# Final sums of the experts' outputs with 64 tokens' two choices on 128 partitions, and the last normalisation on three engines

## The chip, the cores and the metric

One core of a Trainium2 chip. The metric is the device time of one launch in microseconds; the median over the runs counts. All matrices are float32. Engines: PE (TensorE), DVE (VectorE), ACT (ScalarE), POOL (GpSimd) and SP, which issues most DMAs.

## What is computed

One decoder layer for 544 tokens of width 1024: 512 of a prompt and 32 of eight samples, with shared weights. Three mixers (a gated short convolution, a Mamba-2 scan, a cross-attention) are merged and projected, then normalised. The second half is a mixture of 32 experts in 4 groups, two experts per token, and a second normalisation:

```python
    x = layer_norm(ALPHA * x + mix, ln1_g[l], ln1_b[l])
    ffn = hier_moe(x.reshape(b * L, D_MODEL), ...)
    x = layer_norm(ALPHA * x + ffn, ln2_g[l], ln2_b[l])
...
    # hier_moe, its end
    out = lax.map(expert_block, (buf.reshape(n_blocks, MOE_BLOCK, D_MODEL), block_expert)).reshape(-1, D_MODEL)
    y = jnp.sum(out[dest].reshape(T, EXP_TOPK, D_MODEL).astype(f32) * gate[..., None], axis=1)
```

So every token's result is ALPHA times its own row of x, plus gate 0 times the output of its first expert, plus gate 1 times that of its second, normalised over its 1024 columns: minus the mean, over the standard deviation, times ln2_g, plus ln2_b. ALPHA is 2 to the power of one quarter.

## The kernel before

The kernel is written by hand, one program per engine, with semaphores between them. Tokens lie in five tiles: tiles 0 to 3 with 128 prompt tokens each, tile 4 with the 32 samples' tokens. The stages in order are: a stream of weight slabs, each split into a high and a low part (ACT and DVE) for three PE products; the scan; the cross-attention; the output projection with the first normalisation; the router; the experts; the final sum and second normalisation.

**Router.** DVE works out gates, slots and indices (to L2250). It signals gi_v (indices for POOL's gathers), slot_v (what SP and later the other engines read), and gate_v (gates, for ACT). `gate[:, t, k]` is the gate of token t*128 + p for its choice k.

**Experts.** There are 64 fixed blocks of 32 tokens (NB0 = 64) over 32 experts, and 28 more that are skipped unless an expert gets more tokens than planned. An expert's weights are two halves of w1 (2 MB each) and w2 (2 MB). SP loads them one expert after another into three places of `arena`: fetch1 (L545) waits until PE has done the gate products (gu_mm) of the expert three before, fetch2 (L551) until it has done its down products (dn_mm). Per block POOL gathers the tokens' rows (L1542, an indirect DMA), PE transposes them (turn_x, L1074), ACT copies them (L1468), PE multiplies by w1 (gate_up, L1090: 32 instructions in four column sets of 32), ACT computes the SiLU (L1473), DVE the product (hidden, L2258), PE turns it (turn_h, L1097), DVE copies (L2262), PE multiplies by w2 (down, L1109), DVE copies (L2268), and POOL scatters (L1554) into ybuf in DRAM. ybuf has four rows of 256 columns for each pair of token and choice, pair 2*token + choice.

After the copies of the third block ACT writes `gd`, eleven matrices of 128x128 (L1484, L1485): for every tile and choice the identity with its rows scaled by that gate, and the identity times ALPHA. PE needs them only behind the last block.

**The end.** SP waits for ov_p, which POOL raises when all scatters have landed (L1589), and then loads each tile from ybuf with one token's two outputs side by side on a partition, 8 KB (L603, into yld); the fifth load waits until PE has used a slot, since four semaphores serve five tiles. PE forms each half of a tile (512 columns, one PSUM bank) as three products in one sum: ALPHA identity times x (own_part, L1138), gate 0 times the first output (L1154), gate 1 times the second (L1155). An fp32 matmul appears as two passes in the records. Own parts of tiles 0 and 1 come before ov_p, those of tiles 2 and 3 behind it, the one of tile 4 when DVE has read tile 0 from PSUM. Then, per tile in the order 0 to 4:

```python
                    c_.done(v.bn_stats(lstat[0:n, t, half], pair_[:, half]))          # L2295, twice
                v.bn_aggr(lmv[0:n, t], ...).then_inc(Z["f_a"], 1)                     # L2297
                v.scalar_tensor_tensor(halves(x1[0:n, t]), pair_, lmv[0:n, t, 0:1], halves(lnw2[0:n, 0]), ALU.subtract, ALU.mult)  # L2302
                c_.done(v.reciprocal(lrs[0:n, t:t + 1], lsd[0:n, t:t + 1]))           # L2305
                v.scalar_tensor_tensor(x1[0:n, t], x1[0:n, t], lrs[0:n, t:t + 1], lnw2[0:n, 1], ALU.mult, ALU.add)                 # L2308
```

All five are DVE's. ACT gives the standard deviation in between (a square root of one column, L1502). SP stores each tile when f_p says that it is done (L608). SP's order is: all loads, then all stores.

Of the kernel before, what the change touches and what calls it, by code (L numbers as in the profile page):

```python
# [69 lines left out]
W1S, W2S = KT * D, FF // P * D  # L70
SKIP = 2048
# [5 lines left out]
C_QUAD, C_SKIP, C_PART, C_KEYC, C_CAP, C_START, C_VAL, C_MEAN = 790, 791, 792, 793, 794, 795, 798, 800  # L77
# [28 lines left out]
def build(nc, A):  # L106
    with ExitStack() as ctx:
# [187 lines left out]
        yld = place("yld", [P, TT, 2 * D], F32, r_hi)  # L295
        gd = place("gd", [P, 2 * TT + 1, P], F32, tmp_at)
# [6 lines left out]
        raw_half = sem("raw_half")  # L303
        w_hi = sem("w_hi")
# [23 lines left out]
                 "g_in0 g_in1 g_in2 g_in3 sc_out0 sc_out1 cur cur_ov fin_in0 fin_in1 fin_in2 fin_in3 gate_v gd_a f_mm f_v f_a f_sd f_p f_st ov_p on").split()  # L328
# [35 lines left out]
        def _(sp_):  # L364
# [250 lines left out]
        def _(pe):  # L615
# [496 lines left out]

            turn_x(0, 0)
# [3 lines left out]
            for n_ in range(1, NB0):  # L1117
# [4 lines left out]
                turn_h(n_)  # L1122
            down(NB0 - 1)
# [36 lines left out]
        def _(act):  # L1160
# [338 lines left out]
            for t in range(TT):  # L1499
                n = min(T, t * P + P) - t * P  # L1500
                act.wait_ge(Z["f_a"], t + 1)
                nc.scalar.activation(lsd[0:n, t:t + 1], lmv[0:n, t, 1:2], ACT.Sqrt, bias=small[0:n, 41:42]).then_inc(Z["f_sd"], 1)  # L1502


        @block.gpsimd
        def _(pool):
# [82 lines left out]
            pool.sem_inc(Z["ov_p"], 1)  # L1589


        @block.vector
        def _(dve):
# [655 lines left out]
            dve.sem_inc(Z["slot_v"], 1)  # L2249
            dve.sem_inc(Z["gate_v"], 1)  # L2250
# [39 lines left out]
            for t in range(TT):  # L2290
                n = min(T, t * P + P) - t * P
                pair_ = ps[0:n, 2 * (t % 4):2 * (t % 4) + 2, :]
                for half in range(2):
                    dve.wait_ge(Z["f_mm"], 2 * t + half + 1)
# [3 lines left out]
                dve.wait_ge(Z["f_a"], t + 1)  # L2298
# [137 lines left out]
```

## Time and profile before

| | |
|---|---|
| time, median of 3 runs | 1616.73 us |
| runs | 1616.74, 1616.73, 1613.91 us |
| span of the profiled execution, first to last instruction | 1610.5 us |
| mean granted clock of TensorE | 0.964 |
| PE busy | 1487.6 us, 92% |
| DVE busy | 691.9 us, 43% |
| ACT busy | 453.1 us, 28% |
| POOL busy | 176.2 us, 11% |
| DMA moved | 368.25 MB, mean 229 GB/s |
| chain that ended last | PE 72%, DMA 18%, DVE 5%, ACT 2% |

The profile gives no time of the profiled execution other than its span; the median of the runs is 6.2 us longer than that span. Times in views are microseconds from the start of the span, durations of single instructions in groups are ns. "x" is a count of instructions, "idle before" the time in which the engine had nothing to do ahead of them, with what ended it; the granted clock is a share of 2.4 GHz. DMA share is the mean busy share of the 16 DMA engines.

### The profile page before, as it was taken

The numbers are of one execution on the slowest core, as the hardware profiler recorded it, in microseconds if no ns is written. First come the engines' busy times: TensorE is split into PE (matmuls) and PEld (weight loads), VectorE is DVE, ScalarE is ACT, GpSimd is POOL, SyncE is SP. The second block draws the span as 40 slices with busy tenths as digits, with TensorE's granted clock in tenths as the row PEclk, the third lists the DMA queues.
The fourth block names the chain that finished last, engine by engine and source line by source line (L and its number), as shares of the span: only waits on it lengthen the run. The fifth ranks groups of instructions, "written<-read, shape, count | busy, mean of one in ns | idle before, by whom it ended". The sixth has DMA issues, their size and how long they took to land.

```text
span 1610.5 us, 34696 instructions
## 1 busy us (share of the span) xinstructions
PE 1487.6 (92%) x14388; PEld 1194.2 (74%) x14388; DVE 691.9 (43%) x1227; ACT 453.1 (28%) x874; POOL 176.2 (11%) x356
## 2 busy tenths in 40 slices
PE   7999999999899999999999989958987887898897
PEld 7999999999788999999988769744543443444443
DVE  5766666676679572223444325562111111111115
ACT  4534553544222452123343333112100000000000
POOL 1100000000000000000000000003423232333320
PEclk9999999999899999999999999978989998999989
DMA  5223354344448323252355453775999999999994
GB/s 201 75 82 92 115 160 151 113 126 157 152 149 298 116 80 102 83 216 91 118 194 189 177 220 99 285 331 221 418 423 423 420 422 421 397 403 420 420 409 177
DMA packets 86849, 368.25 MB, mean 229 GB/s; under 512 B 14296, under 2 KB 37536, under 8 KB 71712
## 3 DMA queue, kind: packets, MB, share of 16 engines
q1 hardware_dynamic: 80576, 357.37, 58.5%
q0 software_dynamic: 6144, 8.95, 1.5%
q8 instruction: 106, 1.74, 0.4%
q14 instruction: 23, 0.19, 0.0%
HBM read 344.81 MB, written 29.31 MB: 232 GB/s over the span
## 4 chain that ended last, share of the span: by engine, by line
PE 72%; DMA 18%; DVE 5%; ACT 2%; issue 2%; SPq 1%; DVEq 0%; POOLq 0%; POOL 0%; ACTq 0%
PE ps L628 35%; DMA arena<-in_w 16%; PE ps L1090 8%; PE ps L772 5%; PE ps L1109 4%; PE ps L986 3%; PE ps L877 3%; PE ps L859 3%; PE ps L723 1%; PE ps L720 1%; PE ps L909 1%; PE ps L888 1%; PE ps L1074 1%; DVE wl L1604 1%; PE ps L713 1%
## 5 line engine op out<-in xcount | busy, mean ns | idle before, releaser
L1090 PE MATMUL ps<-arena,xT 128*32 128x256 f32 x4096 | 259.5, 406 | 62.6 <-DMA arena<-in_w 62.0
L1604 DVE TENSOR_TENSOR wl<-raw,wh 128x1024 fp32r<-128x1024 f32 x151 | 183.4, 1222 | 169.2 <-ACT wh L1167 168.9
L1090 PEld LDWEIGHTS ps<-arena,xT 128*32 128x32 f32 x4096 | 133.3, 116 | 164.9 <-issue 51.8
L628 PE MATMUL ps<-xh,wh 128*128 128x272 f32 x1136 | 243.6, 296 | 3.2 <-DVE wl L1604 2.0
L628 PE MATMUL ps<-xh,wl 128*128 128x272 f32 x1136 | 235.0, 288 | 0.0
L628 PE MATMUL ps<-xl,wh 128*128 128x272 f32 x1136 | 234.2, 288 | 0.0
L628 PEld LDWEIGHTS ps<-xh,wh 128*128 128x128 f32 x1136 | 179.1, 188 | 14.1 <-issue 9.7
L628 PEld LDWEIGHTS ps<-xl,wh 128*128 128x128 f32 x1136 | 178.4, 188 | 0.0
L628 PEld LDWEIGHTS ps<-xh,wl 128*128 128x128 f32 x1136 | 177.4, 189 | 0.0
L1167 ACT ACTIVATE wh<-raw 128x1024 fp32r<-128x1024 f32 x151 | 158.1, 1055 | 38.7 <-PE ps L986 20.7
L2258 DVE TENSOR_TENSOR hbuf<-sg,ps 128x128 f32<-128x128 f32 x64 | 18.4, 288 | 311.7 <-ACT sg L1473 311.7
L1473 ACT ACTIVATE sg<-ps 128x128 f32<-128x128 f32 x64 | 17.8, 278 | 422.1 <-PE ps L1090 422.1
L1109 PE MATMUL ps<-arena,hTb 128*32 128x256 f32 x2048 | 124.6, 384 | 1.1 <-DMA arena<-in_w 1.1
L1526 POOL MEMSET xg<- 128x256 f32 x4 | 1.1, 312 | 890.8 <-PE ps L986 890.8
L1109 PEld LDWEIGHTS ps<-arena,hTb 128*32 128x32 f32 x2048 | 60.5, 110 | 45.6 <-issue 11.7
L1179 ACT ACTIVATE tmp<-ps 128x544 f32<-128x544 f32 x56 | 34.6, 617 | 191.5 <-PE ps L628 180.2
L2268 DVE COPY yb<-ps 128x256 f32<-128x256 f32 x64 | 27.2, 425 | 112.0 <-PE ps L1109 112.0
L1554 POOL DMA_INDIRECT ybuf_dram<-yb,curs x64 | 65.6, 1025 | 59.1 <-POOL curs L1551 55.7
L1542 POOL DMA_INDIRECT xg<-x_dram,curg x60 | 62.8, 1047 | 51.0 <-POOL curg L1536 51.0
L772 PE MATMUL ps<-xh,wh 128*128 128x272 f32 x256 | 55.3, 298 | 0.0
L772 PE MATMUL ps<-xl,wh 128*128 128x272 f32 x256 | 53.3, 290 | 0.0
L772 PE MATMUL ps<-xh,wl 128*128 128x272 f32 x256 | 53.1, 289 | 0.0
(408 smaller groups left out, 2348.7 us busy)
## 6 DMA issues: line engine op xcount, KB each, us to landing
arena<-in_w SPq DMA_DIRECT2D x96, 2048.0 KB, 30.5
raw<-in_slabs SPq DMA_DIRECT2D x151, 512.0 KB, 4.3
bc<-acs_dram SPq DMA_DIRECT2D x16, 512.0 KB, 5.8
hs<-in_h SPq DMA_DIRECT2D x16, 512.0 KB, 5.2
out_h_sample<-hs SPq DMA_DIRECT2D x16, 512.0 KB, 4.8
kv<-in_kT SPq DMA_DIRECT2D x8, 1024.0 KB, 4.9
kv<-in_vc SPq DMA_DIRECT2D x4, 1024.0 KB, 7.1
kvx<-in_vc SPq DMA_DIRECT2D x2, 2048.0 KB, 11.0
```

Of the source, the lines that this page charges most:

```text
L628: r = nc.tensor.matmul(ps[:, 2 * (ub % 2) + half, 0:HT], w[:, s, col], x[:, koff + kk, half * HT:half * HT + HT], start=first and kk == 0 ...
L772: r = nc.tensor.matmul(ps[:, 2 * (u % 2) + half, 0:HT], w[:, b % RING, kk * P:kk * P + P], x[:, kk, half * HT:half * HT + HT], start=kk == ...
L859: r = nc.tensor.matmul(ps[:, 4 * what + 2 * m + half, :], a[:, kk, m * P:m * P + P], w[:, b % RING, half * 512:half * 512 + 512], start=kk ...
L877: r = nc.tensor.matmul(ps[:, 2 * (u % 2) + half, 0:HT], w[:, b % RING, kk * P:kk * P + P], x[:, kk, half * HT:half * HT + HT], start=kk == ...
L986: r = nc.tensor.matmul(ps[0:n, bank, :], a[:, k, t * P:t * P + n], w[:, b % RING, kq * 512:kq * 512 + 512], start=k == 0 and n_ == 0, stop ...
L1090: r = nc.tensor.matmul(ps[QS * c:QS * c + QS, 2, 0:2 * FQ], xT[:, s, kk % 2, kk // 2 * QS:kk // 2 * QS + QS], arena[:, at_:at_ + 2 * FQ], ...
L1109: r = nc.tensor.matmul(ps[QS * q_:QS * q_ + QS, 5, 0:QD], hTb[:, QS * c:QS * c + QS], arena[:, at_:at_ + QD], start=c == 0, stop=c == NQ - 1)
L1167: nc.scalar.activation(wh[:, b % RING], raw[:, b % RING], ACT.Copy).then_inc(w_hi, 1)
L1179: nc.scalar.activation(tmp[:, ub % RING, 0:T].rearrange("p (h t) -> p h t", h=2), pair(ub), func).then_inc(evac, 1)
L1542: nc.gpsimd.indirect_dma_start(out=xg[s][:], out_offset=None, in_=A["x1d"], in_offset=bass.IndirectOffsetOnAxis(ap=gidx[:, s:s + 1] if cnt ...
L1554: nc.gpsimd.indirect_dma_start(out=A["ybuf"], out_offset=bass.IndirectOffsetOnAxis(ap=curs[:, s:s + 1], axis=0), in_=yb[:, s], in_offset=N ...
L1604: v.tensor_tensor(wl[:, s], raw[:, s], wh[:, s].bitcast(F32), ALU.subtract).then_inc(w_lo, 1)
```

## The change

The order of tiles in the end is now 4, 0, 1, 2, 3 (LAST), everywhere: loads, own parts, sums, normalisation, stores. ybuf is read as pairs: 128 partitions hold both choices of 64 tokens (2 x 64 pairs), in two groups per tile, with 4 KB each. A sum over a token's two choices is then one product with 128 rows and 64 columns; the two groups of a tile write to PSUM partitions 0 to 63 and 64 to 127. For the 32 samples one group with 64 rows and 32 columns is enough. The five loads have semaphores of their own (four that were used at the start of the kernel, and raw_half), and the fifth waits for nothing.

The matrix for it has the gate of pair r in row r and column r // 2. DVE writes its transpose (gl), in five instructions between slot_v and gate_v; PE transposes it (five transposes, behind turn_h of block 1); ACT copies the result from PSUM (two copies) and writes the ALPHA identity.

Of the normalisation, DVE keeps statistics, the first pass and the reciprocal. For the first four tiles in order ACT multiplies by the reciprocal (in place) and POOL adds ln2_b; for the last tile DVE does both in one pass as before, once POOL's four adds are done.

```diff
+PG = P // 2
+LAST = (TT - 1, *range(TT - 1))
...
-        yld = place("yld", [P, TT, 2 * D], F32, r_hi)
-        gd = place("gd", [P, 2 * TT + 1, P], F32, tmp_at)
+        yld = place("yld", [P, TT, 2, D], F32, r_hi)
+        gd = place("gd", [P, TT + 1, P], F32, tmp_at)
+        gl = place("gl", [P, TT, P], F32, tmp_at + 4 * (TT + 1) * P)
+        fin_in = [*x_in, raw_half]
...
         # SP
-            for t in range(TT):
-                if t >= 4:
-                    sp_.wait_ge(Z["f_mm"], 2 * (t - 3))
-                n_ = min(T, t * P + P) - t * P
-                sp_.dma_start(yld[0:n_, t], rows(A["ybuf"].rearrange("(t k) d -> t (k d)", k=2 * NQ), t)
-                              ).then_inc(Z[f"fin_in{t % 4}"], 16)
-            for t in range(TT):
-                sp_.wait_ge(Z["f_p"], t + 1)
+            for i, t in enumerate(LAST):
+                pairs_ = A["ybuf"].rearrange("(p q) d -> p (q d)", q=NQ)[2 * t * P:2 * min(T, t * P + P)]
+                if t < TT - 1:
+                    sp_.dma_start(yld[:, t], pairs_.rearrange("(g p) d -> p g d", p=P)).then_inc(fin_in[i], 16)
+                else:
+                    sp_.dma_start(yld[0:2 * SAMP, t, 0], pairs_).then_inc(fin_in[i], 16)
+            for i, t in enumerate(LAST):
+                sp_.wait_ge(Z["f_p"], i + 1)
...
         # PE
+            def turn_gates():
+                pe.wait_ge(Z["gate_v"], 1)
+                for t in range(TT - 1):
+                    nc.tensor.transpose(ps[:, 6, t * P:t * P + P], gl[:, t], ident)
+                nc.tensor.transpose(ps[0:2 * SAMP, 7, 3 * P:3 * P + SAMP], gl[0:SAMP, TT - 1, 0:2 * SAMP], ident[0:SAMP, 0:SAMP]
+                                    ).then_inc(Z["gt_mm"], 1)
...
                 turn_h(n_)
+                if n_ == 1:
+                    turn_gates()
...
-            for t in range(TT):
+            for i, t in enumerate(LAST):
                 n = min(T, t * P + P) - t * P
-                pe.wait_ge(Z[f"fin_in{t % 4}"], 16 * (t // 4 + 1))
-                if t >= 4:
-                    pe.wait_ge(Z["f_v"], t - 3)
-                    own_part(t)
+                if i >= 4:
+                    pe.wait_ge(Z["f_v"], i - 3)
+                    own_part(i)
+                pe.wait_ge(fin_in[i], 32)
                 for half in range(2):
-                    out, c = ps[0:n, 2 * (t % 4) + half, :], half * 512
-                    nc.tensor.matmul(out, gd[0:n, 2 * t, 0:n], yld[0:n, t, c:c + 512], start=False, stop=False)
-                    nc.tensor.matmul(out, gd[0:n, 2 * t + 1, 0:n], yld[0:n, t, D + c:D + c + 512], start=False, stop=True
-                                     ).then_inc(Z["f_mm"], 1)
+                    c = half * 512
+                    for r0 in range(0, n, PG):
+                        m = min(PG, n - r0)
+                        r = nc.tensor.matmul(ps[r0:r0 + m, 2 * (i % 4) + half, :], gd[0:2 * m, t, r0:r0 + m],
+                                             yld[0:2 * m, t, r0 // PG, c:c + 512], start=False, stop=True)
+                    r.then_inc(Z["f_mm"], 1)
...
         # ACT
-            for t in range(TT):
-                for k in range(2):
-                    nc.scalar.activation(gd[:, 2 * t + k], ident, ACT.Copy, scale=gate[:, t, k:k + 1])
-            nc.scalar.activation(gd[:, 2 * TT], ident, ACT.Copy, scale=ALPHA).then_inc(Z["gd_a"], 1)
+            act.wait_ge(Z["gt_mm"], 1)
+            nc.scalar.activation(gd[:, 0:TT - 1], ps[:, 6, :].rearrange("p (t q) -> p t q", q=P), ACT.Copy)
+            nc.scalar.activation(gd[0:2 * SAMP, TT - 1, 0:SAMP], ps[0:2 * SAMP, 7, 3 * P:3 * P + SAMP], ACT.Copy)
+            nc.scalar.activation(gd[:, TT], ident, ACT.Copy, scale=ALPHA).then_inc(Z["gd_a"], 1)
...
                 nc.scalar.activation(lsd[0:n, t:t + 1], lmv[0:n, t, 1:2], ACT.Sqrt, bias=small[0:n, 41:42]).then_inc(Z["f_sd"], 1)
+                if i < TT - 1:
+                    act.wait_ge(Z["f_v"], i + 1)
+                    act.wait_ge(Z["f_r"], i + 1)
+                    nc.scalar.activation(x1[0:n, t], x1[0:n, t], ACT.Copy, scale=lrs[0:n, t:t + 1]).then_inc(Z["f_n"], 1)
...
         # POOL
+            for i, t in enumerate(LAST[:-1]):
+                n = min(T, t * P + P) - t * P
+                pool.wait_ge(Z["f_n"], i + 1)
+                nc.gpsimd.tensor_tensor(x1[0:n, t], x1[0:n, t], lnw2[0:n, 1], ALU.add).then_inc(Z["f_p"], 1)
...
         # DVE, between slot_v and gate_v
+            for t in range(TT):
+                c_.done(v.scalar_tensor_tensor(gl[:, t].rearrange("p (m k) -> p m k", k=2),
+                                               riota[:, 0, 0:PG].unsqueeze(2).to_broadcast([P, PG, 2]), cst[:, C_OWN:C_OWN + 1],
+                                               gate[:, t].unsqueeze(1).to_broadcast([P, PG, 2]), ALU.is_equal, ALU.mult))
+            c_.sync()
...
         # DVE, per tile
-                c_.done(v.reciprocal(lrs[0:n, t:t + 1], lsd[0:n, t:t + 1]))
-                c_.sync()
-                dve.wait_ge(Z["f_v"], t + 1)
-                v.scalar_tensor_tensor(x1[0:n, t], x1[0:n, t], lrs[0:n, t:t + 1], lnw2[0:n, 1], ALU.mult, ALU.add
-                                       ).then_inc(Z["f_p"], 1)
+                v.reciprocal(lrs[0:n, t:t + 1], lsd[0:n, t:t + 1]).then_inc(Z["f_r"], 1)
+                if i == TT - 1:
+                    dve.wait_ge(Z["f_r"], i + 1)
+                    dve.wait_ge(Z["f_v"], i + 1)
+                    dve.wait_ge(Z["f_p"], i)
+                    v.scalar_tensor_tensor(x1[0:n, t], x1[0:n, t], lrs[0:n, t:t + 1], lnw2[0:n, 1], ALU.mult, ALU.add
+                                           ).then_inc(Z["f_p"], 1)
```

## Rows read from the trace of the kernel before

**Rows 1.** The page's slices: busy tenths of the DMA engines, 40.3 us a slice

```profile
DMA  5223354344448323252355453775999999999994
```

**Rows 2.** Windows: stretch, length, busy of each engine, clock, DMA share, GB/s

```profile
1107.00:1108.00 1.00, 1.00 (x21) 0.42 (x13) 0.00 (x0) 1.00 (x5) 0.00 (x0) 1.00 0.82 197
1108.00:1109.00 1.00, 1.00 (x17) 0.57 (x21) 0.62 (x2) 1.00 (x4) 0.00 (x1) 1.00 1.01 418
...
1400.00:1410.00 10.00, 10.00 (x169) 5.43 (x165) 1.37 (x6) 1.00 (x4) 4.27 (x8) 1.00 0.74 304
```

**Rows 3.** Timeline of the tail: start, duration, engine, line, operation [idle before]

```profile
1579.37 8.88 SPq L603 DMA_DIRECT2D yld<-ybuf_dram  x5
...
1579.39 3.70 PE L1138 MATMUL ps<-x,gd 128*128 128x512 f32 x8 [0.21 <-POOLq L1589]
...
1584.19 1.12 PE L1154 MATMUL ps<-yld,gd 128*128 128x512 f32 x2 [1.10 <-DMA yld<-ybuf_dram]
...
1586.21 0.70 DVE L2295 BATCH_NORM_STATS2 lstat<-ps 128x6 f32<-128x512 f32 x1 [10.18 <-PE ps L1155]
```

**Rows 4.** Chain that ended last, in order of time: start, duration, what

```profile
1587.93 0.71 DVE lstat L2295
...
1590.27 0.04 issue
...
1591.59 1.22 DVE lstat L2295 x2
...
1593.07 1.28 DVE x L2302
1594.36 0.08 DVE lrs L2305
...
1595.75 1.22 DVE lstat L2295 x2
...
1606.90 1.27 DVE x L2308
```

**Rows 5.** DMA issues of the tail: count, KB each, median us to landing

```profile
out_y<-x SPq DMA_DIRECT2D x4, 512.0 KB, 2.6
...
out_y<-x SPq DMA_DIRECT2D x1, 128.0 KB, 1.9
```

**Rows 6.** Timeline where the expert stage starts

```profile
1101.46 0.29 DVE L2258 TENSOR_TENSOR hbuf<-sg,ps 128x128 f32<-128x128 f32 x1 [7.82 <-ACT sg L1473]
...
1105.93 0.88 SPq L545 DMA_DIRECT2D arena<-in_w  x2
...
1114.24 0.33 SPq L551 DMA_DIRECT2D arena<-in_w  x1
```

**Rows 7.** Groups by line and form (busy us, mean ns); last, one line's instructions

```profile
L1536 POOL COPY curg<-gidx 128x1 int32 x60 | 11.8, 196 | 0.0
...
L1516 POOL COPY tmp<-cvprev 128x24 f32 x24 | 9.1, 380 | 18.9 <-DMA sprev<-in_sprev 18.2 <-issue 0.7
...
L1526 POOL MEMSET xg<- 128x256 f32 x4 | 1.1, 312 | 890.8 <-PE ps L986 890.8
...
L1167 ACT ACTIVATE wh<-raw 128x1024 fp32r<-128x1024 f32 x151 | 158.1, 1055 | 38.7 <-PE ps L986 20.7 <-PE ps L859 14.9 <-DMA raw<-in_slabs 3.1
...
L1442 ACT ACT_TABLE_LOAD  x1: 1283/1283/1283, 1025.5 to 1025.5; - x1
```

**Rows 8.** Chain: column sets of 64 in the scan; start of the expert stage

```profile
210.09 1.02 PE ps L720 x16
...
1105.73 0.37 PE ps L1074 x2
...
1108.22 3.59 PE ps L1090 x64
```

**Rows 9.** Windows where PE waits for weights

```profile
1176.00:1178.00 2.00, 0.00 (x0) 0.00 (x0) 0.00 (x0) 0.00 (x0) 1.22 (x2) 0.92 1.05 434
1178.00:1180.00 2.00, 0.39 (x4) 0.23 (x8) 0.00 (x0) 0.00 (x0) 1.05 (x1) 0.50 1.02 428
```

More of the change, by code:

```diff
@@ L76 @@
 C_STRIS, C_SUFS, C_BM, C_IOTA, C_PRE, C_TOK, C_G = 640, 672, 704, 712, 744, 776, 786
-C_QUAD, C_SKIP, C_PART, C_KEYC, C_CAP, C_START, C_VAL, C_MEAN = 790, 791, 792, 793, 794, 795, 798, 800
+C_QUAD, C_SKIP, C_PART, C_KEYC, C_CAP, C_START, C_OWN, C_VAL, C_MEAN = 790, 791, 792, 793, 794, 795, 796, 798, 800
 CW = 928
@@ L327, in build @@
                  "tab_mm slot_v gi_v xT_mm xT_v gu_mm sil h_v hT_mm hT_v dn_mm y_v srt_v srt_mm "
-                 "g_in0 g_in1 g_in2 g_in3 sc_out0 sc_out1 cur cur_ov fin_in0 fin_in1 fin_in2 fin_in3 gate_v gd_a f_mm f_v f_a f_sd f_p f_st ov_p on").split()
+                 "g_in0 g_in1 g_in2 g_in3 sc_out0 sc_out1 cur cur_ov gate_v gd_a gt_mm f_mm f_v f_a f_sd f_r f_n f_p f_st ov_p on").split()
         Z = {n_: sem("z_" + n_) for n_ in names}
@@ L1132, in _, with own_part @@
                     down(NB0, ob)
-            def own_part(t):
+            def own_part(i):
+                t = LAST[i]
                 n = min(T, t * P + P) - t * P
@@ L1137, in own_part @@
                     c = half * 512
-                    nc.tensor.matmul(ps[0:n, 2 * (t % 4) + half, :], gd[0:n, 2 * TT, 0:n], x1[0:n, t, c:c + 512], start=True, stop=False)
+                    nc.tensor.matmul(ps[0:n, 2 * (i % 4) + half, :], gd[0:n, TT, 0:n], x1[0:n, t, c:c + 512], start=True, stop=False)
             pe.wait_ge(Z["gd_a"], 1)
@@ L1498, in _ @@
                     silu(NB0, ob, 1)
-            for t in range(TT):
+            for i, t in enumerate(LAST):
                 n = min(T, t * P + P) - t * P
-                act.wait_ge(Z["f_a"], t + 1)
+                act.wait_ge(Z["f_a"], i + 1)
                 nc.scalar.activation(lsd[0:n, t:t + 1], lmv[0:n, t, 1:2], ACT.Sqrt, bias=small[0:n, 41:42]).then_inc(Z["f_sd"], 1)
+                if i < TT - 1:
+                    act.wait_ge(Z["f_v"], i + 1)
+                    act.wait_ge(Z["f_r"], i + 1)
+                    nc.scalar.activation(x1[0:n, t], x1[0:n, t], ACT.Copy, scale=lrs[0:n, t:t + 1]).then_inc(Z["f_n"], 1)
         @block.gpsimd
@@ L2288, in _ @@
                     y_copy(NB0, 1, ob, 1, ix(16 * (NB0 // 2), ob, 16))
-            for t in range(TT):
+            for i, t in enumerate(LAST):
                 n = min(T, t * P + P) - t * P
-                pair_ = ps[0:n, 2 * (t % 4):2 * (t % 4) + 2, :]
+                pair_ = ps[0:n, 2 * (i % 4):2 * (i % 4) + 2, :]
                 for half in range(2):
-                    dve.wait_ge(Z["f_mm"], 2 * t + half + 1)
+                    dve.wait_ge(Z["f_mm"], 2 * i + half + 1)
                     c_.done(v.bn_stats(lstat[0:n, t, half], pair_[:, half]))
@@ L2297, in _ @@
                 v.bn_aggr(lmv[0:n, t], lstat[0:n, t].rearrange("p h s -> p (h s)")).then_inc(Z["f_a"], 1)
-                dve.wait_ge(Z["f_a"], t + 1)
+                dve.wait_ge(Z["f_a"], i + 1)
                 dve.wait_ge(Z["x1_st"], 16 * TT)
@@ L2303, in _ @@
                                        ).then_inc(Z["f_v"], 1)
-                dve.wait_ge(Z["f_sd"], t + 1)
-                c_.done(v.reciprocal(lrs[0:n, t:t + 1], lsd[0:n, t:t + 1]))
-                c_.sync()
-                dve.wait_ge(Z["f_v"], t + 1)
-                v.scalar_tensor_tensor(x1[0:n, t], x1[0:n, t], lrs[0:n, t:t + 1], lnw2[0:n, 1], ALU.mult, ALU.add
-                                       ).then_inc(Z["f_p"], 1)
+                dve.wait_ge(Z["f_sd"], i + 1)
+                v.reciprocal(lrs[0:n, t:t + 1], lsd[0:n, t:t + 1]).then_inc(Z["f_r"], 1)
[5 more added lines that the diff above has]
+                                           ).then_inc(Z["f_p"], 1)
 SHAPES = {"mk": (MEM, D), "mv": (MEM, D), "snew": (P, KT, NSEQ + 1, 2), "cvnew": (P, CT, NSEQ + 1, 3),
@@ L2383 @@
     cst[:, C_PART] = np.arange(P)
+    cst[:, C_OWN] = np.arange(P) % PG
     cst[:NE, C_KEYC] = NE - np.arange(NE) - 64 * pre
```

## The prediction

> **What bounds it now.** I read the page first: the row of the DMA engines stands at 9 from slice 29 to slice 39 and is near it from slice 25 on, and has no cover of its own at the end [rows 1]. The windows over the expert stage say the same: the weight stream starts at 1107 us, and from 1108 on the 16 DMA engines are full, 1.01 at 418 GB/s; the one dip is 0.74 around 1405 us [rows 2]. PE waits for weights now and then. Work on PE, DVE or ACT is free in this stage as long as SP can issue each weight load before the queue runs dry. After the stream comes a tail that nothing covers, up to 1610.5; I went through it in the timeline and in the chain of waits.
>
> In the tail SP issues the loads of the experts' outputs at 1579.37; PE starts eight passes of own products at 1579.39, 0.43 each (3.70 for eight, the last one's end modelled 0.27 behind), and is free at 1582.81. It starts the first final products at 1584.19, when 1 MB has landed; DVE's first statistics start at 1586.21 [rows 3]. From there the chain is DVE alone: two statistics (1.22), the aggregate, a first pass over the tile (1.28), the reciprocal (0.08), a second pass (1.28). The period is 1595.75 - 1591.59 = 4.16 us, and the samples' tile with its 32 rows costs as much: its last pass takes 1.27 [rows 4]. PE needs eight passes, 3.42, a tile and is ahead. The last pass ends at 1608.17, the samples' store (128 KB) lands 1.9 after its issue [rows 5], and the span ends 2.35 after that pass. So **the tail is bound by DVE's five turns of 4.16 us**, behind a head that waits for a load.
>
> **The change, part by part.**
>
> Expert stage, DVE: five instructions of 128 outputs make gl, behind slot_v, for which SP and PE wait. The nearest row is the hidden product, 128x128 in 0.29: 1.5 us. DVE is idle for 7.82 us there [rows 6]. Nothing on the path.
>
> Expert stage, ACT: ten scaled copies and a plain one go; three copies come, 128x512, 64x32 and 128x128, together less than one of 128x1024 (1.055) and 0.4 [rows 7]. They wait for the transposes now, and the next SiLU stands behind them; it needs a whole gate product first, which PE starts behind the transposes and which takes 3.59 [rows 8]. The product covers them.
>
> Expert stage, PE: five transposes. The chain gives two of them 0.37 [rows 8], so 0.93, where PE has no gap. What hides it is the stream. The load issued at 1105.93 is asked for before the transposes; it reaches full rate at about 1107.5, and its 4 MB last until about 1117.4. The next one, issued at 1114.24, comes at 1115.2; with the 1.6 us from issue to full rate its bytes flow from 1116.8 [rows 2, 6]. The cover is 0.6 us. PE's lateness ends in its first wait for weights. I take nothing; without the cover it is at most 0.93 us.
>
> Tail, loads: the samples' tile is first, 256 KB instead of 1 MB, and the fifth load waits for no slot. 1 MB landed at 1584.15 or just before, 4.8 after issue; 0.79 MB less at 0.42 MB/us leaves 2.9, and stores of 128 and 512 KB land in 1.9 and 2.6 [rows 2, 3, 5]. So it lands between 1581.3 and 1582.3, before PE is free. The runs are 4 KB instead of 8 KB, as in the stores, which land in 2.6. I count no loss; one of 10% in 4.25 MB would be 1 us, and the later tiles have more slack than that.
>
> Tail, head: PE starts at 1582.81, 1.38 earlier. Half of the samples' tile is one instruction of two passes, 0.85. The statistics start 0.31 behind a half's last pass (1586.21 - 1584.19 - 4 x 0.43), so the second ones at 1582.81 + 1.71 + 0.31 = 1584.83. From second statistics to the end of the reciprocal rows 4 have 1590.27 - 1587.93 = 2.34. **R0**, DVE's end with the first tile, is 1587.17.
>
> Tail, two column sets: each half has two instructions of 64 columns. The only such rows are 16 passes of 128*64 with 128 columns in 1.02 us; one after the other they would take 16 x 0.107 = 1.71, so the ratio is 0.60 [rows 8]. Of two ends, 0.85 and 1.71 for a half, I take 0.60 x 1.71 = 1.02. (Four sets of 32 do better: 64 passes of 256 columns in 3.59, serial 13.7.) Tile 0 lands 256 KB later than now, at 1584.8; its halves are ready for DVE at 1586.1 and 1587.2, DVE wants them at 1587.2 and 1587.8. From there PE needs 2.0 a tile and DVE is the bound.
>
> Tail, DVE: the second pass leaves it for four tiles, so the period is 4.16 - 1.29 = 2.87; R3 = 1587.17 + 3 x 2.87 = 1595.78 and R4 = 1598.65.
>
> Tail, ACT: a copy of 128x1024 with a tensor as scale; 1.055 without one, and I take 1.15. The first normalisation has square roots and copies side by side on one table load [rows 7]. ACT is done 1.2 behind R, its next square root is wanted 1.46 behind R: no delay.
>
> Tail, POOL: an add of two 128x1024 tiles. **No row shows it.** A memset of 128x256 takes 0.312, so 1.25 for 1024 columns, and 1.0 if some of it is fixed: the low end. Three streams at that rate are 3.75, and the copies, 0.196 for one column and 0.380 for 24 in runs of three, give 8.2 at 8 ns a column, the high end [rows 7]. I take twice the memset, 2.5: two tiles are read, one is written, and the memset is the row with long runs. The Trainium skill's GPSIMD Engine Reference, section 3.1, speaks against this place for the work: a two-input add of 2048 columns measured 4497 ns there against 2293 on VectorE. As an estimate that is 2.25 us here, and the sum would be 0.25 shorter. No run here shows it yet.
>
> Sum: the fourth add ends at 1595.78 + 1.2 + 0.05 + 2.5 = 1599.53. DVE's last pass has to wait for it (f_p), 0.85 beyond R4; it runs to 1600.84. The last store is 512 KB, 2.6 instead of 1.9, so the span ends 3.05 behind: **1603.9** against 1610.5, a gain of 6.6. The page gives the span of the profiled execution and no other time of it; the median of the runs, 1616.73, lies 6.2 above that span, and the runs spread over 2.8. With the same 6.2: 1610.1.
>
> **Rivals.**
>
> *The sets don't run side by side.* PE then needs 3.42 a tile: 1584.8 + 3 x 3.42 + 1.71 (the fifth own part) + 3.42 = 1600.2; statistics to reciprocal add 0.31 + 2.34, the last pass and the store 4.37: 1607.2, a gain of 3.3, 1613.4. Rows 8 speak against it. *The clock falls* to 1.2 GHz (0.50): side by side a tile costs 4.1, the own part 3.4, the end is 1611.6 and the time 1617.8. It fell to 0.50 where PE had no work in the whole window before [rows 9]; the gaps that I forecast are below 1 us. Chances 0.06 and 0.03.
>
> *DVE's first pass is shut out by POOL's add*, the case that ends slower. Place: the add of a tile runs from R + 1.25 to R + 3.75, and DVE's next first pass would start at R + 1.5. If it waits for the add, the period is 1.25 + p + 1.28 + 0.1 = 5.13 with p = 2.5, R4 is 1607.7, the end 1612.1: 1618.3. It decides from p = 2.1 on and costs more than 0.2% from 2.9. For it: no row shows work of this size on both. Against it: the first pass reads PSUM and one tile of SBUF. The Trainium skill's page SBUF — State Buffer, section Who interferes with whom, has this as a lock between a DVE instruction with two SBUF inputs and a GpSimd instruction that reads SBUF; by its rule the first pass stays clear, and the last pass, which has two, waits for the adds anyway. Chance 0.06.
>
> *The add is just dear.* It is the bound from 2.87 on: at 3.75 the fourth ends at 1588.4 + 15.2 = 1603.6 and the span at 1608.0 (gain 2.5, 1614.2); at 4.4 the gain is gone; at 8.2 the time is 1632. Chance of more than 3.6: 0.05.
>
> *The change does nothing*: only if DVE weren't the bound; the stream behind the transposes can take back 0.93 of 6.6 and no more.
>
> **How the numbers follow.** Forecast 0.80; rivals 0.06, 0.03, 0.06, 0.05. The forecast's own bounds: an add of 1.0 removes the last wait (0.85 less) and the runs scatter by 1.4 or so either way, 1607.8; above, the stream's 0.93 and an add of 3.6 come to 1613.6, by the serial case's 1613.4. I give 1607.6 to 1614.0. 0.2% is 3.2 us, about what a measurement of this kernel can tell from no change. Faster by more: the forecast nearly whole and half of the serial case, 0.81. Slower by more: lock or add with a high price, 0.07. Within: 0.12.
>
> **What would show it.** Right: final products from 1.4 us earlier; statistics every 2.87 us; passes of 128*64 in pairs, about 1.0 a half; an add of 2.0 to 3.0; DVE's last pass about 0.9 behind its reciprocal, waiting for POOL; DMA full around 1117. Wrong: DVE's first pass idle behind POOL; a clock of 0.50 before the last tile; a hole in the stream at 1117; a table load between square root and copy.

## The result, and the profile after

The changed kernel takes **1607.68 us** in the median of five runs (1605.5 to 1611.21), the kernel before 1616.73 in its five beside them (1613.91 to 1618.62): a ratio of 0.9945, 95% interval 0.993 to 0.9961. The forecast was 1610.1; 9.1 us came where 6.6 were expected, and the median lies only 0.08 above the lower end of the range (1607.6 to 1614.0). With 5.7 us between the fastest and the slowest of the five runs, it is partly luck that it lies inside. The profiled execution has a span of 1604.3 and took 1606.3 by itself, so the two are 2.0 apart, where the prediction took 6.2.

The profile's page of the changed kernel, sections 1 and 2:

```profile
PE 1478.1 (92%) x14389; PEld 1187.8 (74%) x14389; DVE 688.4 (43%) x1228; ACT 455.2 (28%) x870; POOL 185.6 (12%) x360
...
DMA  5222455344538332362355363775999999999995
```

The digits of the last ten slices are those of before [rows 1] but for the very last (5 instead of 4): no new dip. POOL has 9.4 us more (its four adds), DVE 3.5 less. The rest is in the tail. Its timeline in the changed kernel answers to [rows 3, 4]; the line numbers are those of the new file (L1152 own parts, L1170 products over the experts' outputs, L2324 statistics, L2331 first pass, L1522 ACT's scaled copy, L1613 POOL's add, L2339 the last pass):

```profile
1579.83 0.50 SPq L608 DMA_DIRECT2D yld<-ybuf_dram  x1
1579.86 3.70 PE L1152 MATMUL ps<-x,gd 128*128 128x512 f32 x8 [1.94 <-POOLq L1609]
...
1583.49 1.90 PE L1170 MATMUL ps<-yld,gd 64*32 64x512 f32 x4
...
1585.43 0.69 DVE L2324 BATCH_NORM_STATS2 lstat<-ps 32x6 f32<-32x512 f32 x1 [0.17 <-PE ps L1170]
1585.83 1.94 PE L1170 MATMUL ps<-yld,gd 128*64 128x512 f32 x8 [0.43 <-DMA yld<-ybuf_dram]
...
1587.65 1.26 DVE L2324 BATCH_NORM_STATS2 lstat<-ps 128x6 f32<-128x512 f32 x2
1587.82 1.15 ACT L1522 ACTIVATE x<-x,lrs 32x1024 f32<-32x1024 f32 x1 [1.14 <-DVE lrs L2334]
...
1589.05 2.36 POOL L1613 TENSOR_TENSOR x<-x,lnw 32x1024 f32<-32x1024 f32 x1 [12.30 <-ACT x L1522]
...
1590.46 1.28 DVE L2324 BATCH_NORM_STATS2 lstat<-ps 128x6 f32<-128x512 f32 x2
...
1593.29 1.27 DVE L2324 BATCH_NORM_STATS2 lstat<-ps 128x6 f32<-128x512 f32 x2
...
1596.11 1.30 DVE L2324 BATCH_NORM_STATS2 lstat<-ps 128x6 f32<-128x512 f32 x2
...
1597.52 2.34 POOL L1613 TENSOR_TENSOR x<-x,lnw 128x1024 f32<-128x1024 f32 x1 [0.46 <-ACT x L1522]
...
1598.89 0.15 DVE L2334 RECIPROCAL lrs<-lsd 128x1 f32<-128x1 f32 x1
1599.99 1.28 DVE L2339 SCALAR_TENSOR_TENSOR x<-x,lrs,lnw 128x1024 f32<-128x1024 f32 x1 [0.95 <-POOL x L1613]
```

To be seen: from the second tile on the statistics start 2.81 to 2.83 apart instead of 4.16; PE delivers a tile in 1.94 and then waits for the next load; POOL is idle 0.46 before each later add, and DVE waits for it once, 0.95 at the very end; the end comes 3.03 behind the last pass. I call **tail** what lies between SP's first load of ybuf (1579.83) and the end of the span: 24.5 us, against 1610.5 - 1579.37 = 31.1 before. The forecast was 24.5.

Where the expert stage starts, the new work and SP's issues behind it (timeline), and the windows over the stream there, which answer to [rows 2, 6]:

```profile
1104.06 0.88 SPq L549 DMA_DIRECT2D arena<-in_w  x2
...
1106.18 0.60 PE L1120 MATMUL ps<-cst,gl 128*128 128x128 f32 x4
...
1112.95 0.33 SPq L555 DMA_DIRECT2D arena<-in_w  x1
```

```profile
1116.00:1117.00 1.00, 1.00 (x18) 0.42 (x14) 0.03 (x1) 0.28 (x1) 0.47 (x1) 1.00 0.95 393
1117.00:1118.00 1.00, 1.00 (x20) 0.57 (x24) 0.26 (x1) 0.38 (x1) 0.58 (x1) 1.00 1.12 475
1118.00:1119.00 1.00, 1.00 (x17) 0.40 (x9) 0.10 (x1) 0.00 (x0) 0.00 (x0) 1.00 0.85 360
```

SP's third load comes 8.89 behind the first two instead of 8.31, and the stream has no hole.

### The profile page after: what moved, and what is told of

It is laid out like the page before. It is cut to its first block, busy times and chain, and to the rows that moved or that the text cites. A ratio compares the mean times of both kernels' runs of the same rounds, so it can differ in the third digit from the quotient of the medians.

```text
span 1604.3 us, 34701 instructions
## 1 busy us (share of the span) xinstructions
PE 1478.1 (92%) x14389; PEld 1187.8 (74%) x14389; DVE 688.4 (43%) x1228; ACT 455.2 (28%) x870; POOL 185.6 (12%) x360
## 4 chain that ended last, share of the span: by engine, by line
PE 73%; DMA 18%; DVE 4%; ACT 2%; issue 2%; SPq 1%; POOLq 0%; POOL 0%; DVEq 0%; ACTq 0%
PE ps L632 35%; DMA arena<-in_w 16%; PE ps L1094 8%; PE ps L776 5%; PE ps L1113 4%; PE ps L990 3%; PE ps L881 3%; PE ps L863 3%; PE ps L727 1%; PE ps L724 1%; PE ps L913 1%; PE ps L892 1%; PE ps L1078 1%; DVE wl L1628 1%; PE ps L717 1%
```

## The experiments

The tail's length is read from each run's profile (one execution); the ratio compares the times over five rounds with those of the kernel before beside them. Where a run has one time only, no ratio is given. My theory A was throughout that the tail is the sum of the prediction, each term where it was put; the rivals stand in the expectations.

**The changed kernel once more.** Expected: 

> The changed kernel once more. The tail, from SP's issue of the first load of the experts' outputs to the end of the span, was 31.1 us in the kernel before and 24.5 in the changed one, 6.6 less; the median of five runs fell by 9.05. Theory A: all that the change gives is in the tail, 6.6, and the other 2.4 are scatter of the stages ahead of it (the runs of before spread over 4.7). Then this ratio lies between 0.995 and 0.997 and the tail at 24.5. Rival: the change also gains in an earlier stage. Then the ratio is again 0.9945 or less, and the span up to the tail is again more than 1.5 us shorter in the median.

1609.69 us beside 1617.51 for the kernel before; ratio 0.9948, interval 0.9934 to 0.9962. The gain is there again, a little larger than the 0.995 to 0.997 of my theory A. The tail of the profiled execution, however, is 27.9 instead of 24.5. The rival isn't borne out either: the tail starts at 1580.28, later than the 1579.37 of the kernel before. Over all 13 profiles of this document the tail starts between 1577.7 and 1584.25, in the mean at 1580.2 in the four of kernels without transposes of the gates and at 1580.7 in the nine of kernels with them. So no profile shows a gain ahead of the tail. The timeline of this execution, and windows over the same stretch:

```profile
1588.58 7.07 PE L1170 MATMUL ps<-yld,gd 128*64 128x512 f32 x24 [2.75 <-DMA yld<-ybuf_dram]
1590.34 0.70 DVE L2324 BATCH_NORM_STATS2 lstat<-ps 128x6 f32<-128x512 f32 x1 [2.17 <-PE ps L1170]
...
1592.04 0.70 DVE L2324 BATCH_NORM_STATS2 lstat<-ps 128x6 f32<-128x512 f32 x1 [1.01 <-PE ps L1170]
```

```profile
1586.00:1588.00 2.00, 0.00 (x0) 0.00 (x0) 1.93 (x3) 0.29 (x1) 0.00 (x0) 1.00 1.02 418
1588.00:1590.00 2.00, 1.42 (x4) 0.44 (x6) 0.17 (x2) 1.15 (x1) 0.51 (x1) 0.72 1.02 416
1590.00:1592.00 2.00, 2.00 (x8) 0.65 (x6) 0.70 (x1) 0.00 (x0) 1.83 (x1) 0.50 1.03 414
```

Tile 0 landed late here; PE had nothing for 2.75 us, and right after it the granted clock goes to 0.50 (1.2 GHz). DVE waits 2.17 for the first half and 1.01 more for the second. Of these 3.2 the clock makes about 1.5 by my estimate: at full clock the first statistics come 1.13 behind PE's start and the second 0.86 later (1588.63, 1589.76 and 1590.62 in the run in the order 0 to 4 below), here they come 1.76 behind it and 1.70 later. From then on the period is 2.83 again. So the head of the tail varies from one execution to the next, and a single profile can't be compared with another to better than some 3 us.

**The kernel before once more.** Expected: 

> The kernel before, profiled again. Its shown profile has a tail of 31.1 us (issue of the first load to the end), with the first 1 MB in 4.8 us after issue. Three comparisons gave 8.4 to 9 us where that profile and the changed one give 6.6 in the tail. Theory L: the shown profile was a favourable execution; the first 1 MB lands later as a rule (6.7 in the run with the normalisation alone), PE idles past 1585 and its clock falls. Then the first load lands 6 us or more behind its issue here and the tail is 33 us or more. Rival: the tail is 31.1 again and the further 2 us are from ahead of it, or scatter.

One time of 1617.62 with a span of 1615.4 (2.2 apart), and a tail of 32.85: nearer to theory L's 33 than to the rival's 31.1. PE's first product over the experts' outputs, and the statistics of the last tile; then windows over PE's last products, with the granted clock as third number from the right:

```profile
1582.55 9.66 SPq L603 DMA_DIRECT2D yld<-ybuf_dram  x5
...
1588.15 1.12 PE L1154 MATMUL ps<-yld,gd 128*128 128x512 f32 x2 [1.87 <-DMA yld<-ybuf_dram]
...
1607.50 1.91 PE L1155 MATMUL ps<-yld,gd 32*32 32x512 f32 x2
...
1609.45 0.69 DVE L2295 BATCH_NORM_STATS2 lstat<-ps 32x6 f32<-32x512 f32 x1 [0.83 <-PE ps L1155]
```

```profile
1604.00:1606.00 2.00, 2.00 (x5) 0.49 (x4) 1.93 (x4) 0.29 (x1) 0.00 (x0) 0.82 0.64 260
1606.00:1608.00 2.00, 2.00 (x3) 0.35 (x2) 1.96 (x4) 0.00 (x0) 0.00 (x0) 0.50 0.01 2
```

The first 1 MB came 5.6 behind its issue instead of 4.8 (theory L had 6), and at the samples' tile two passes take 1.91 instead of 1.02: the granted clock fell to 0.50 from about 1605 on, while PE was busy without a gap, with products of 32 rows and 32 columns since 1602.08. DVE waits 0.83 for them. In the execution that the prediction rests on the same products kept the full clock, and the load was early. Its span of 1610.5, with 2.2 on top, is a time of about 1612.7, below all five runs of before beside the changed kernel. But the tail is the smaller part of this: of the 4.9 between the two spans 1.75 lie in the tail and 3.2 ahead of it (it starts at 1582.55 instead of 1579.37).

**Only the normalisation on three engines** (sums and order as before). The main lines; DVE's second pass stays for the last tile only, and the loads signal other semaphores.

```diff
+                if t < TT - 1:
+                    act.wait_ge(Z["f_v"], t + 1)
+                    act.wait_ge(Z["f_r"], t + 1)
+                    nc.scalar.activation(x1[0:n, t], x1[0:n, t], ACT.Copy, scale=lrs[0:n, t:t + 1]).then_inc(Z["f_n"], 1)
...
+            for t in range(TT - 1):
+                pool.wait_ge(Z["f_n"], t + 1)
+                nc.gpsimd.tensor_tensor(x1[:, t], x1[:, t], lnw2[:, 1], ALU.add).then_inc(Z["f_p"], 1)
```

Expected: 

> Only the three-engine normalisation on the kernel before: natural order, two products of 128 columns per half. Theory A: DVE would need 2.85 a tile, but PE's four serial products need 3.42, so PE becomes the bound: 4.8 to the first landing, 4 x 3.42, the fifth own part 1.71, 3.42, then 0.3 + 2.3 + 1.3 + 2.35: tail 29.9 us, 1.2 less than before. Rival: DVE's passes alone set the tail, so taking four of 1.29 away gives 5.2: 25.9 us.

Ratio 0.9995, interval 0.9981 to 1.0009: no gain that can be told from none. Its timeline:

```profile
1587.94 1.81 PE L1154 MATMUL ps<-yld,gd 128*128 128x512 f32 x2 [2.94 <-DMA yld<-ybuf_dram]
...
1596.81 0.70 DVE L2302 BATCH_NORM_STATS2 lstat<-ps 128x6 f32<-128x512 f32 x1 [0.51 <-PE ps L1155]
...
1600.24 0.70 DVE L2302 BATCH_NORM_STATS2 lstat<-ps 128x6 f32<-128x512 f32 x1 [0.51 <-PE ps L1155]
```

The period is 3.43, which is PE's eight passes, and DVE is idle 0.51 before the second statistics of each tile: **PE is the bound as soon as DVE is relieved**. The tail is 33.7 where 29.9 were expected, because the first load took 6.7 to land and the clock fell behind PE's wait of 2.94.

**Only the new sums and the order** (DVE keeps both passes; ACT's scaled copies and POOL's adds, not shown here, go).

```diff
-                if i == TT - 1:
-                    dve.wait_ge(Z["f_r"], i + 1)
...
+                dve.wait_ge(Z["f_r"], i + 1)
+                dve.wait_ge(Z["f_v"], i + 1)
+                v.scalar_tensor_tensor(x1[0:n, t], x1[0:n, t], lrs[0:n, t:t + 1], lnw2[0:n, 1], ALU.mult, ALU.add
+                                       ).then_inc(Z["f_p"], 1)
```

Expected: 

> Only the new sums and the new order: pairs on 128 partitions, column sets, the samples' tile first; the whole normalisation stays on DVE. Theory A: DVE's period stays 4.13, the head is as in the changed kernel (second statistics 5.6 us behind the issue), so the last pass ends at 5.6 + 4 x 4.13 + 2.3 + 1.3 = 25.7 and the tail is 28.7, 2.4 less than before and 4.2 more than the changed kernel. Rival: PE's cheaper sums are worth nothing since DVE was the bound; only the head's 0.8 counts, less 0.7 for the larger last store: tail 31.0.

1613.89 us, ratio 0.9976 (0.9965 to 0.9987), tail 29.2 where 28.7 were expected. Its timeline, two tiles' statistics:

```profile
1591.64 1.29 DVE L2316 BATCH_NORM_STATS2 lstat<-ps 128x6 f32<-128x512 f32 x2
...
1595.80 1.29 DVE L2316 BATCH_NORM_STATS2 lstat<-ps 128x6 f32<-128x512 f32 x2
```

DVE's period stays 4.16, as theory A has it. The sums shorten the head and nothing else while DVE is the bound.

**Only the order 4, 0, 1, 2, 3**, on the kernel before (every index of a slot is the place in the order). Expected: 

> Only the order 4, 0, 1, 2, 3 on the kernel before; products, loads of 8 KB and DVE's two passes as they were. By the steps: second statistics 3.4 + 3.4 + 0.3 = 7.2 us behind the issue instead of 8.6, then 4 x 4.16 + 2.3 + 1.3 and 3.05 for the larger last store: tail 30.5, 0.6 less than the shown profile of before. Theory L: against the typical run of before it gives 2 us or more, ratio 0.9985 or less. Rival: 0.6 us, ratio 0.9995 or more.

1614.01 us, ratio 0.9987 (0.9976 to 0.9997), about 2 us, between the two theories and nearer to L; tail 32.5 instead of 30.5 in the execution profiled. The samples' load landed 4.2 behind its issue, and tile 0's products began at half clock, right behind the samples' 32-column ones and without a gap on PE:

```profile
1585.62 2.08 PE L1156 MATMUL ps<-yld,gd 128*128 128x512 f32 x2
```

**The changed kernel in the order 0 to 4.** `LAST = tuple(range(TT))`. Expected: 

> The changed kernel in the order 0 to 4. The first load is 1 MB again. With a landing at 4.8 us: second statistics at 7.1, R3 18.0, POOL's fourth add to 21.7, DVE's last pass to 23.1, the samples' small store 2.35: tail 25.4, 0.9 more than in the changed kernel. Theory L: the first load lands at 6 or later and PE's clock falls in the wait: tail 27 or more, and the ratio to before 0.9965 or more. Rival: tail 25.4, ratio near 0.9955.

1609.79 us, ratio 0.9959 (0.9945 to 0.9973), tail 26.3. PE went on 6.1 behind the issue of the first load, after a wait of 2.36, but the clock stayed at 1.00; DVE's last pass waited 0.51 for POOL. So theory L is right about the load and wrong about the clock, and tail and ratio lie nearer to the rival's 25.4 and 0.9955 than to its 27 and 0.9965. Against the changed kernel's 0.9945 and 0.9948 the order is worth about 2 us here too. Both values (this one and that of the order alone) agree with each other and with the 1.38 that the prediction has for the head, but the intervals are wider than the difference.

**DVE's last pass doesn't wait for POOL.**

```diff
-                    dve.wait_ge(Z["f_p"], i)
...
-                                           ).then_inc(Z["f_p"], 1)
+                                           ).then_inc(Z["f_l"], 1)
```

(SP waits for f_l before the last store.) Expected: 

> The changed kernel, where DVE's last pass does not wait for POOL's fourth add (it signals a semaphore of its own, which SP waits for ahead of the last store). Theory A, no lock: the last pass starts behind its reciprocal, 0.95 earlier, and runs beside the add: tail 23.5 us. Rival, the lock between a DVE instruction with two SBUF inputs and a GpSimd one that reads SBUF: the pass starts but ends only about 1.3 behind the add, tail 24.4 as now, or the add gets longer than 2.37.

Ratio 0.9957 (0.9941 to 0.9973), tail 1608.7 - 1584.25 = 24.5: the rival's 24.4 and not theory A's 23.5. Its timeline:

```profile
1599.16 2.37 POOL L1613 TENSOR_TENSOR x<-x,lnw 128x1024 f32<-128x1024 f32 x1 [0.46 <-ACT x L1522]
1599.31 1.28 DVE L2331 SCALAR_TENSOR_TENSOR x<-ps,lmv,lnw 128x1024 f32<-128x1024 f32 x1
...
1601.98 2.34 POOL L1613 TENSOR_TENSOR x<-x,lnw 128x1024 f32<-128x1024 f32 x1 [0.46 <-ACT x L1522]
...
1603.57 1.84 DVE L2338 SCALAR_TENSOR_TENSOR x<-x,lrs,lnw 128x1024 f32<-128x1024 f32 x1
```

A first pass, which reads PSUM and one tile of SBUF, takes 1.28 though it lies wholly beside an add; the last pass, which reads two tiles of SBUF, takes 1.84 when it starts 0.75 before the add's end. It ends 1.09 behind the add instead of 1.41 in the changed kernel. So there is next to nothing to gain by taking the wait of 0.95 away: of the 0.75 that this pass lay beside POOL's add it lost 0.56 (1.84 instead of 1.28). The Trainium skill (SBUF — State Buffer, Who interferes with whom) tells the two apart just so: a DVE instruction with at most one input from SBUF doesn't contend with GpSimd, one with two contends with a GpSimd instruction that reads SBUF. This trace agrees with it on both, by 1.28 and 1.84.

**The last pass reads PSUM.** The last tile's first pass leaves its result in PSUM; the last pass then needs only one tile from SBUF, waits for nobody, and is made and stored in halves (SP's two stores are not shown).

```diff
-                v.scalar_tensor_tensor(halves(x1[0:n, t]), pair_, ...)
+                v.scalar_tensor_tensor(halves(x1[0:n, t]) if i < TT - 1 else pair_, pair_, ...)
...
-                    dve.wait_ge(Z["f_p"], i)
-                    v.scalar_tensor_tensor(x1[0:n, t], x1[0:n, t], ...)
+                    for half in range(2):
+                        c = half * 512
+                        v.scalar_tensor_tensor(x1[0:n, t, c:c + 512], pair_[:, half], ...).then_inc(Z["f_l"], 1)
```

Expected: 

> The changed kernel, but the last tile's first pass leaves its result in PSUM, so that the last pass reads PSUM and one tile of SBUF, doesn't wait for POOL's fourth add, and is made and stored in two halves. Theory A (DVE and POOL shut each other out only where DVE reads two tiles of SBUF): both halves run at 0.66 each right behind the reciprocal while POOL's fourth add still runs; the last pass ends 1.35 behind the reciprocal instead of 2.3 (0.95 of waiting gone), and the last store has 256 KB, so the span ends some 2.6 behind it instead of 3.03. The tail (SP's first load to the end) is 24.5 - 0.95 - 0.4 = 23.1 with a samples' load that lands 3.5 behind its issue, and longer by what it lands later. About 1.3 us less than the changed kernel, a ratio of about 0.9945 to the kernel before. Rival B (any DVE pass beside POOL's add is slowed near the end, or PSUM as output is dearer): halves of 0.9 or more, and nothing gained.

1609.56 us, ratio 0.9954 (0.9943 to 0.9966): no different from the changed kernel. The tail is 24.6 where 23.1 were expected. The reciprocal of the last tile ends 19.83 behind SP's first load (1579.99), 0.62 later than in the changed kernel, since the loads landed later and PE fell behind: its products for the last tile start 15.52 behind the first load instead of 14.90. Its timeline, and the DMA issues of the last microseconds:

```profile
1597.87 2.34 POOL L1619 TENSOR_TENSOR x<-x,lnw 128x1024 f32<-128x1024 f32 x1 [0.46 <-ACT x L1528]
...
1599.67 0.15 DVE L2340 RECIPROCAL lrs<-lsd 128x1 f32<-128x1 f32 x1
1599.87 1.41 DVE L2346 SCALAR_TENSOR_TENSOR x<-ps,lrs,lnw 128x512 f32<-128x512 f32 x2
```

```profile
out_y<-x SPq DMA_DIRECT2D x1, 512.0 KB, 2.7
out_y<-x SPq DMA_DIRECT2D x2, 256.0 KB, 2.9
```

The mechanism works: both halves take 1.41 together and start 0.05 behind the reciprocal, the first of them with 0.34 beside POOL's add. But from the reciprocal's end to the end of the span are 4.78, where the changed kernel has 1604.3 - 1599.04 = 5.26: 0.48 saved, not 1.3: the last pass ends 0.77 nearer to the reciprocal, and the end comes 3.3 behind it instead of 3.03. The fourth tile's store (512 KB, issued only when POOL is done, at 1600.2) and the two halves are now underway at once, and the halves land 2.9 behind their issues, later than the 2.6 of 512 KB alone; I had counted on 0.4 less. The end still hangs on DVE's last half: its store, issued at 1601.3, lands at about 1604.2, the fourth tile's at 1602.9. **But that store now has 768 KB before it, issued within the last 1.1 us**; that this makes it slower is my reading, no run takes it apart. And half a microsecond can't be told from nothing in the times.

**POOL's adds made twice** (the first of each two writes to a dead place). Expected: 

> The changed kernel with every one of POOL's adds preceded by one more of the same size into a dead place. Theory A (POOL is behind DVE's 2.85 with room of 0.5, and becomes the bound from there on): POOL needs 4.75 a tile, its four tiles end 19.0 behind the first scaled copy, DVE's last pass waits for them, and the tail is 24.5 + 8.0 = 32.5. Statistics and first passes of DVE keep their 2.85 (they read PSUM). Rival B (POOL's add also holds up DVE's first passes): DVE's period is over 4, and the tail over 34. Rival C (adds are hidden anyway): below 27.

Tail 32.3 (1611.1 - 1578.80) against the 32.5 expected; one time, 1613.09. Timeline, statistics and the last adds:

```profile
1589.60 1.28 DVE L2325 BATCH_NORM_STATS2 lstat<-ps 128x6 f32<-128x512 f32 x2
...
1592.42 1.27 DVE L2325 BATCH_NORM_STATS2 lstat<-ps 128x6 f32<-128x512 f32 x2
...
1604.33 2.33 POOL L1614 TENSOR_TENSOR x<-x,lnw 128x1024 f32<-128x1024 f32 x1
1606.79 1.28 DVE L2340 SCALAR_TENSOR_TENSOR x<-x,lrs,lnw 128x1024 f32<-128x1024 f32 x1 [8.55 <-POOL x L1614]
```

POOL works without a gap and sets the end, and DVE's period stays 2.82 beside it: an add can be too long, but it doesn't hold up DVE's first passes.

**Each product over the experts' outputs made twice.** Expected: 

> The changed kernel with each product over the experts' outputs made twice, so that the experts' part counts double in the result; PE does for each half what it would do if the two column sets ran one after the other. Theory A (side by side is what keeps PE off the bound): PE needs 3.9 a tile, is the bound from the first tile on, DVE is idle about 1.0 before each tile's statistics, and the tail is about 31.3, 6.8 more than in the changed kernel. Rival B (PE has enough slack that DVE or POOL stay the bound): 26 or less.

Tail 30.3 (1611.7 - 1581.44) against 31.3 expected; one time, 1613.7. Timeline, two of the statistics:

```profile
1596.13 0.70 DVE L2324 BATCH_NORM_STATS2 lstat<-ps 128x6 f32<-128x512 f32 x1 [0.51 <-PE ps L1170]
...
1599.56 0.70 DVE L2324 BATCH_NORM_STATS2 lstat<-ps 128x6 f32<-128x512 f32 x1 [0.51 <-PE ps L1170]
```

The period is 3.43, the same as that of the old sums, and rival B's tail of 26 or less is out: this is what the changed kernel would do if the two column sets ran one after the other. I had expected 3.9 by doubling 1.94, but 1.94 holds a last pass's end, modelled; each further pair of passes costs 0.43.

**The four large transposes five times over.**

```diff
+                for _ in range(5):
+                    for t in range(TT - 1):
+                        nc.tensor.transpose(ps[:, 6, t * P:t * P + P], gl[:, t], ident)
```

Expected: 

> The changed kernel with the four large transposes of the gates issued five times over (the result is the same). 16 more at 0.11 to 0.13 us: PE is 1.9 us later behind them. My step said that the stream of weights covers 0.6 us beyond what the transposes take. Then the next load is issued 1.9 later, the windows between 4 MB and 6 MB after the start of the stream show a hole of about 1.3 to 1.5 us in the DMA share, and PE's first wait for weights ends as much later. Rival: the queue holds more than I count and no hole shows.

They take 2.35 instead of 0.60, and SP's next load comes 10.64 behind the first two instead of 8.89. Timeline and windows:

```profile
1106.27 0.90 SPq L549 DMA_DIRECT2D arena<-in_w  x2
...
1108.40 2.35 PE L1121 MATMUL ps<-cst,gl 128*128 128x128 f32 x20
...
1116.91 0.33 SPq L555 DMA_DIRECT2D arena<-in_w  x1
```

```profile
1118.00:1119.00 1.00, 1.00 (x24) 0.65 (x20) 0.00 (x0) 0.00 (x0) 0.57 (x1) 1.00 0.97 217
1119.00:1120.00 1.00, 1.00 (x28) 0.57 (x20) 0.00 (x0) 0.00 (x0) 0.64 (x2) 1.00 0.67 279
```

Now there is a hole: 217 and 279 GB/s where 420 are had, (203 + 141) / 420 = 0.82 us of transfers, where 1.3 to 1.5 were expected (in the DMA share only the second window dips, to 0.67). So of 1.75 us more delay about 0.93 were still covered. PE's first wait for weights shows less still: it ends 74.02 behind SP's first two loads here, 73.70 in the changed kernel and 73.68 in the kernel before (1177.76 - 1104.06, 1179.61 - 1105.93). So the transposes of the changed kernel lie wholly in the cover, and four times as many more let that wait end only some 0.3 later. In the tail of this one execution, 30.3 long, PE started the own parts 2.74 late without a wait that the profile shows, and at half clock; the transposes lie 470 us earlier, and I have no explanation that a run shows. The tail itself says nothing on the cover of the transposes.

## Why the prediction was right, and where it was off

The changes taken apart, each against the runs of the kernel before beside it over five rounds; "about us" is worked out from the ratio. The normalisation alone, the new sums with the order, and the second value for all stand beside the same runs of before, the other rows beside others:

| version | ratio | interval | about us |
|---|---|---|---|
| order alone | 0.9987 | 0.9976 to 0.9997 | -2.1 |
| new sums and order | 0.9976 | 0.9965 to 0.9987 | -3.9 |
| normalisation alone | 0.9995 | 0.9981 to 1.0009 | -0.8 |
| new sums and normalisation, order 0 to 4 | 0.9959 | 0.9945 to 0.9973 | -6.6 |
| all, two comparisons | 0.9945, 0.9948 | 0.993 to 0.9962 | -9, -8.4 |

**The two big parts need each other.** DVE's 4.16 hides PE's 3.43; relieve DVE alone and PE's 3.43 comes out, relieve PE alone and DVE's 4.16 stays. Together the period is 2.82. That is the mechanism of the prediction, and the rows show it.

By the prediction's own steps:

- *DVE is the bound with 2.87 a tile*: 2.81 to 2.83. *ACT's copy 1.15*: 1.15, with no table load between root and copy. *POOL's add 2.5*: 2.34 to 2.37, also where it has 32 rows. The estimate from the Trainium skill's figure (GPSIMD Engine Reference, section 3.1: 4497 ns for 2048 columns) was 2.25; the trace lies between the two, nearer to it.
- *DVE's last pass waits 0.85 for POOL*: 0.95. *End 3.05 behind the pass's end*: 3.03.
- *Two column sets, 1.02 a half*: mis-sized. Eight passes take 1.94 with one modelled end, and where DVE waits for PE, 0.86 lie between the statistics of two halves (1589.76 and 1590.62 in the order 0 to 4). That is 0.43 a pair of passes, fully side by side, not the 0.60 of the scan's rows. It changed nothing, because DVE is the bound; the slack is small, though, since PE also waits for its loads (0.62 a tile), and in the run whose last pass reads PSUM it was PE that held up the last tile.
- *The samples land 2.9 behind the issue at the latest*: mis-sized. They took 3.5, since the DMA engines moved only 106 GB/s in 1580 to 1582; PE waited 0.2 for them. Second statistics came 5.57 behind the own parts' start instead of 5.44.
- *Transposes 0.93, cover 0.6*: five in some 0.75 and a delay of SP's load of 0.58; the cover was larger, 0.93 or more beyond that by the experiment with five times as many. That nothing of it comes out was right: PE's first wait for weights ends where it did (73.70 behind the first loads, 73.68 before).
- *Rivals.* Sets in sequence: excluded by 1.94, and its price by the doubled products. First pass shut out: excluded by 1.28 beside each add; the lock exists, for the last pass. Add too dear: 2.35 is below the period, and the doubled adds show that beyond it POOL does set the end. The clock: I gave 0.03 to a fall of it for the whole tail. In the repeated run it did fall, for some 3.4 us behind a wait of 2.75, and cost about 1.5 us by my estimate above. The prediction's "gaps that I forecast are below 1 us" failed there: it took the landing of a load for a constant.
- *The upper end of the range*: the text puts the stream's 0.93 and an add of 3.6 together at 1613.6. The add alone gives that (1588.42 + 4 x 3.65 + 4.37 + 6.2); with both it would be 1614.5, above the 1614.0 given.

**The step that failed** is the one from span to time: "the median of the runs lies 6.2 above that span", carried over whole. Of these 6.2 only 2.2 lie around the span; the other 4.0 were a favourable execution. Against the one other profile of the kernel before (4.9 longer) 3.2 lie in the stages ahead of the tail and 1.75 in the tail, where the first load landed early and the clock held at the samples' tile. The span forecast, 1603.9, was met (1604.3), and so was the tail. That the span was met takes luck too: the tail starts at 1579.83 in one profile and at 1579.37 in the other, while over all profiles its start scatters by 6.5 us. The gain in the times is about 2 us larger than 6.6. What these 2 us are made of is not settled: the repeated profile of before loses 1.75 at two places that the change touches, the first load of 1 MB and the samples' 32-column products at the end, and the order alone gives 2.1 where its head was sized at 1.38; but the changed kernel's tail varies as well, and the intervals are too wide to book the rest.

## What to carry to other kernels

When a stage has two engines close together (here 4.16 and 3.43 us a tile), a change that relieves the slower one is worth only the distance to the second; cost both edits alone and together before dropping either. GpSimd can take half of an elementwise pass off VectorE, provided that its instruction is shorter than the period (here 2.35 against 2.82) and that VectorE's passes beside it read at most one operand from SBUF. And before a span is turned into a time, look at what of the profiled execution is luck: a load without cover, and a clock that may fall behind PE's wait for it, make the head of such a tail vary by 3 us here, and the stages ahead of it scatter by 6.5.

## What the runs showed of the hardware that was not expected

- VectorE's scalar_tensor_tensor of 128x1024 took 1.28 us beside a GpSimd add when it read PSUM and SBUF, 1.84 when it read two SBUF tiles and overlapped the add's last 0.75 us.
- The GpSimd add of 1024 columns costs 2.36 us with 32 partitions as with 128.
- The granted clock fell to 0.50 right after PE had waited 2.75 us for a load, in two others after 2.94 (for a load) and after 2.74 without work (no cause shown); after waits of 2.36, 1.87 and, in [rows 3], 1.10 it did not. It also fell twice with PE busy throughout, during or right behind the samples' products of 32 rows and 32 columns.
- A first load of 1 MB, issued at the same place, let PE go on 4.8, 5.6, 6.1 and 6.7 us later in four executions of three kernels; a first load of 256 KB landed 3.4 to 4.2 behind its issue in nine.
- Splitting the last store did not shorten the way from the last pass to the end (3.3 us instead of 3.03): its halves of 256 KB, behind 512 KB issued just before, landed in 2.9 us each, where a whole one of 512 KB took 2.6.
